# Where the second layer's w_ada tiles are loaded and summed: in passes A and B alone

## What is computed

```python
for l in range(DEPTH):
    mod = jnp.einsum('bd,dn->bn', cond, w_ada[l]) + b_ada[l]          # cond = silu(c), w_ada[l]: 1024 x 6144
    sh1, sc1, g1, sh2, sc2, g2 = [m[:, None, :] for m in jnp.split(mod, 6, axis=-1)]
    h = rms_norm(x, norm1[l]) * (1.0 + sc1) + sh1
    x = x + g1 * token_mixer(h, ...)                                  # three attention branches, gates, w_out
    h = rms_norm(x, norm2[l]) * (1.0 + sc2) + sh2
    x = x + g2 * swiglu(h, w_gu[l], w_down[l])
```

## Time and profile before

| | |
|---|---|
| median of 3 runs | 994.08 us (994.02 to 995.42) |
| the profiled execution's own time | 991.47 us |
| its span in the profile | 989.3 us |
| PE busy | 935.7 us (95%) |
| DVE busy | 694.0 us (70%) |
| ACT busy | 482.7 us (49%) |
| mean granted clock of PE | 0.976 of full |
| read from HBM | 196.24 MB |

### The profile page before, as it was taken

The page is one execution under the profiler, slowest core; times in us unless marked ns, Lnnn a source line. Parts: engine busy times, 40 slices in busy tenths (PEclk is TensorE's granted clock), DMA queues, the critical chain, the costliest instruction groups (busy, mean ns, idle before and its releaser), DMA issues.

```text
span 989.3 us, 15954 instructions
## 1 busy us (share of the span) xinstructions
PE 935.7 (95%) x6744; PEld 880.1 (89%) x6744; DVE 694.0 (70%) x1087; ACT 482.7 (49%) x654; POOL 24.4 (2%) x49
## 2 busy tenths in 40 slices
PE   8998989998998999999989998999989899999998
PEld 6787969976987999999978997898779799999998
DVE  4997889787784656666574797988878555656443
ACT  4554776455445433343463468374553454333341
POOL 1010000000000000000000000000000000000000
PEclk8999999999998999999989999999999789999999
DMA  9979633414652776767545795251454434654541
GB/s 361 384 285 373 238 114 132 171 44 171 255 213 86 256 255 216 280 237 281 181 170 183 273 327 187 92 204 45 172 211 173 171 128 171 218 207 172 178 164 43
DMA packets 29593, 198.31 MB, mean 200 GB/s; under 512 B 3282, under 2 KB 3794, under 8 KB 7507
## 3 DMA queue, kind: packets, MB, share of 16 engines
q1 hardware_dynamic: 23474, 155.22, 43.6%
q0 software_dynamic: 5760, 41.95, 11.5%
q10 hardware_dynamic: 288, 0.14, 0.0%
HBM read 196.24 MB, written 1.05 MB: 199 GB/s over the span
## 4 chain that ended last, share of the span: by engine, by line
PE 62%; DVE 24%; ACT 7%; issue 4%; DMA 3%; ACTq 0%; DVEq 0%
PE bank L479 16%; PE bank L481 16%; PE bank L480 16%; DVE w_lo L1174 7%; ACT w_hi L873 2%; DVE front L1181 2%; DVE score L1346 2%; DMA raw<-in_slabs_dram 2%; DVE acc L1437 2%; PE bank L506 1%; PE bank L586 1%; PE bank L585 1%; PE bank L587 1%; DVE score L1364 1%; ACT acc L1083 1%
## 5 line engine op out<-in xcount | busy, mean ns | idle before, releaser
L1174 DVE TENSOR_TENSOR w_lo<-raw,w_hi 128x2048 fp32r<-128x2048 f32 (+2 forms) x146 | 314.6, 2160 | 138.7 <-ACT w_hi L873 137.1
L479 PE MATMUL bank<-h_hi,w_hi 128*128 128x256 f32 x1216 | 350.8, 289 | 12.1 <-DVE w_lo L1174 6.2
L873 ACT ACTIVATE w_hi<-raw 128x2048 fp32r<-128x2048 f32 (+2 forms) x146 | 262.9, 1806 | 175.0 <-PE bank L481 120.9
L481 PE MATMUL bank<-h_hi,w_lo 128*128 128x256 f32 x1216 | 347.2, 286 | 0.0
L480 PE MATMUL bank<-h_lo,w_hi 128*128 128x256 f32 x1216 | 347.2, 285 | 0.0
L479 PEld LDWEIGHTS bank<-h_hi,w_hi 128*128 128x128 f32 x1216 | 236.5, 194 | 16.7 <-issue 14.9
L480 PEld LDWEIGHTS bank<-h_lo,w_hi 128*128 128x128 f32 x1216 | 236.5, 195 | 0.1
L481 PEld LDWEIGHTS bank<-h_hi,w_lo 128*128 128x128 f32 x1216 | 236.4, 194 | 0.0
L479 PE MATMUL bank<-y_hi,w_hi 128*128 128x256 f32 x480 | 135.6, 282 | 2.2 <-DVE w_lo L1174 2.2
L480 PE MATMUL bank<-y_lo,w_hi 128*128 128x256 f32 x480 | 135.1, 282 | 0.0
L481 PE MATMUL bank<-y_hi,w_lo 128*128 128x256 f32 x480 | 135.0, 281 | 0.0
(11 more groups left out here) (171 smaller groups left out, 1151.2 us busy)
## 6 DMA issues: line engine op xcount, KB each, us to landing
raw<-in_slabs_dram SPq DMA_DIRECT2D x124, 1024.0 KB, 5.1
front<-in_ada_dram POOLq DMA_DIRECT2D x31, 1024.0 KB, 5.7
acc<-in_ada_dram POOLq DMA_DIRECT2D x9, 1024.0 KB, 5.7
raw<-in_slabs_dram SPq DMA_DIRECT2D x16, 552.0 KB, 4.9
front<-in_ada_dram SPq DMA_DIRECT2D x5, 1024.0 KB, 11.4
raw<-in_slabs_dram SPq DMA_DIRECT2D x6, 768.0 KB, 6.7
proj<-in_ada_dram SPq DMA_DIRECT2D x2, 1024.0 KB, 9.1
x_t<-in_x_dram SPq DMA_DIRECT2D x2, 512.0 KB, 5.3
```

The costliest lines, as they stand in the source:

```text
L479: nc.tensor.matmul(b_out, st_hi, mv_hi, start=start, stop=False, skip_group_check=True)
L481: return nc.tensor.matmul(b_out, st_lo, mv_hi, start=False, stop=stop, skip_group_check=True)
L873: nc.scalar.activation(w_hi[:, n % RING, 0:w], raw[:, n % RING, 0:w], ACT.Copy).then_inc(hi_ready.sem, 1)
L1174: nc.vector.tensor_tensor(w_lo[:, n % RING, 0:w], raw[:, n % RING, 0:w], w_hi[:, n % RING, 0:w], ALU.subtract).then_inc(lo_ready.sem, 1)
```

## The change

The first layer keeps its order. In the second layer the twelve `A_B` tiles are summed after S_A+2, S_A+3, ... S_A+7 (one each, and one more after the last), S_B, S_B+1, S_B+2, S_B+3 and S_B+5, and nowhere else. They go through all three places in turn. POOL loads all twelve as places come free, with no wait for a head. ACT's wait ahead of its squares into `acc` asks for all twelve sums (before: for six).

```diff
-    ADA_SEQ += [(*_tiles[i], i % 3) for i in range(6)] + [(*_tiles[i], i % 2) for i in range(6, 12)]
+    ADA_SEQ += [(*t, i % 2 if _l == 0 and i >= 6 else i % 3) for i, t in enumerate(_tiles)]
@@ POOL
-                for _ in range(10):
+                for _ in range(12 if l else 10):
                     load_ada(n)
                     n += 1
-                pool.wait_ge(scored.sem, scored.at(l, B_HEADS + A_HEADS))
-                for _ in range(2):
-                    load_ada(n)
-                    n += 1
+                if l == 0:
+                    pool.wait_ge(scored.sem, scored.at(l, B_HEADS + A_HEADS))
+                    for _ in range(2):
+                        load_ada(n)
+                        n += 1
@@ ACT
-                act.wait_ge(ada_used.sem, KT + (24 if l else 0) + 6)
+                act.wait_ge(ada_used.sem, KT + (24 + 12 if l else 6))
@@ DVE, second layer (the branch l > 0)
                     for k in range(2, KT):
                         lo(l, S_A + k)
+                        ada_next()
+                    ada_next()
@@ DVE, both layers: the same for the calls after S_B+7, S_GATE0, S_GATE0+1, S_UQ+1 and S_UQ+2
                 lo(l, S_B + 7)
-                ada_next()
+                if l == 0:
+                    ada_next()
@@ DVE, the heads
-                    if n in (15, 17):
+                    if l == 0 and n in (15, 17):
                         ada_next()
```

## The result

The changed kernel takes 985.63 us (median of 10 runs, 984.11 to 989.99) against 994.05 us (10 runs, 990.88 to 997.10): ratio 0.9918, interval 0.9902 to 0.9934, or 8.2 us faster, where 4.8 were forecast. The time lies 1.1 us under the stated range. The profiled execution's own time is 985.63 us, its span 983.6, so 5.8 under the one profiled before.

A forecast was written before the change was run, and what follows sets the result against it. PE was taken as the bound (62% of the chain, DVE 24%), so DVE savings count only where PE waits for DVE, directly or through ACT. 3.2 + 1.6 = 4.8 us off 994.08 gives 989.2 us, range 986.7 to 991.8.

The forecast's parts named there:

- the seven sums: Second layer's pass A: seven sums of 2.41 us fit DVE's waits, hidden by PE's matmuls, at cost 0.
- my two bounds: Pass A transfers, 13.6 MB: 34.3 us at 395 GB/s, or 37.6 us at 362 GB/s; cost 0 either way.
- Behind S_UQ+1: From S_B+7 to S_UQ+2: removed sums let the second pair sum start earlier, gaining 3.2 us (bounds 0.8 and 4.8).
- In the heads: End of the heads: without step 15's sum PE's wait before the last transposes goes, gaining 1.6 us (bounds 1.4 and 2.4).
- The sum of step 17: Heads: it stands ahead of the last y_lo and w_lo of S_BR+1, wanted only at 738.5; removing it gains nothing.
- The rival of slow transfers: Pass A: transfers at 285 GB/s outlast the margin of 4.0 us, giving 999.0 us; chance 0.05.
- behind ACT and its own transfer, not behind the sum: At S_GATE0: w_lo, needed at 580.9, waits for these, so the first three removed sums give nothing.
- no longer compete with slabs, which only helps: After 561 us: tiles leave the DMA queues to slabs; no gain was counted for it.
- by 3.22 as a whole: Indexer heads, DVE full to 662: the chain of DVE behind ACT moves 3.22 us earlier, PE's gates with it.
- Behind it PE is full to 765, and DVE's merging follows PE: After the sum of step 17: PE has no gap to 765 us and DVE follows it; no further gain counted.
- more than the sum: Rival: all of three sums counts, 7.2 us, because ACT's order slackens too, giving 986.9 us; chance 0.08.
- the rival's: Changed kernel with norm idle matmuls plus four before the branches: the four's earlier cost had another cause, 984.5 us, ratio 0.9905.

The follow-up runs named there:

- x_h17: Kernel before with only the sum of head step 17 moved to pass A, that of step 15 staying: 992.05 us, ratio 0.9989.
- x_gates: Kernel before with only the sums behind S_B+7, S_GATE0 and S_GATE0+1 moved to pass A: 992.75 us, ratio 0.9995.
- after_delay: Changed kernel with four idle PE matmuls ahead of the second layer's branch projections: 989.29 us, ratio 0.9958 to the kernel before.
- after_again: The changed kernel as it is, run again beside the kernel before: 984.78 us, ratio 0.9911.
- before_p1: The kernel before, unchanged, run for a second profile: 994.65 us.
- x_uq: Kernel before with only the sums behind S_UQ+1 and S_UQ+2 moved to pass A: 990.01 us, ratio 0.9957.
- x_h15: Kernel before with only the sum of head step 15 moved to pass A, that of step 17 staying: 988.6 us, ratio 0.9965.
- before_p2: The kernel before, unchanged, run for a third profile: 989.63 us.
- heads_fill: Kernel before with idle matmuls around the second norm and only the two heads' sums moved: 983.61 us, ratio 0.9900 to the kernel before.

## Why the prediction was wrong

**Right, step by step.** Pass A took the seven sums for nothing; DVE's queue ran as laid out (w_lo of S_A+6 to S_A+7 5.34 us apart, the last with 0.64 us idle), the transfers at 378 GB/s, between my two bounds, and no PE gap. The 358 GB/s that the Trainium skill gives for HBM reads of one core ("DMA: Bandwidth & Descriptors", section "Where 436 GB/s comes from") is passed here by 6% over 34 us. Behind S_UQ+1 I had 3.2 us, the trace has 3.27, with ACT's w_hi of S_UQ+2 the next to be late, as worked out (DVE waits 1.71 for it). In the heads I had 1.6, the trace 1.48. The sum of step 17 was worth nothing, as x_h17 bears out. The rival of slow transfers did not come.

**Missed, small.** At S_GATE0 I read "behind ACT and its own transfer, not behind the sum", and priced at nothing that tiles "no longer compete with slabs, which only helps". The slab's transfer was the wait. ACT's w_hi of the two gate slabs, before and after:

```profile
575.82 1.92 ACT L873 ACTIVATE w_hi<-raw 128x2048 fp32r<-128x2048 f32 x1 [2.78 <-DMA raw<-in_slabs_dram]
580.74 1.92 ACT L873 ACTIVATE w_hi<-raw 128x2048 fp32r<-128x2048 f32 x1 [3.00 <-DMA raw<-in_slabs_dram]
```
```profile
575.97 1.92 ACT L875 ACTIVATE w_hi<-raw 128x2048 fp32r<-128x2048 f32 x1 [1.87 <-PE bank L607]
579.20 1.92 ACT L875 ACTIVATE w_hi<-raw 128x2048 fp32r<-128x2048 f32 x1 [1.32 <-PE bank L607]
```

From the first scaling of this layer's first norm to the copies of the latents it is 79.8 to 82.3 us (mean 80.8) in the eleven traces with the gates' sums in place and 79.2 to 80.1 (mean 79.8) in the six without: 0.5 in the first pair, 1.0 on the mean, where my sum has 0. By the ratio of x_gates it is 0.5 us, which cannot be told from 0. The other small one is a loss. PE, past the fifth indexer head 3.7 us earlier by its own place, stands longer at the transposes behind the indexer, and falls to the lower clock there:

```profile
PE bank L663 <- ACT acc L1048: 2.8, 1, 2.8
```
```profile
626.00:636.00 10.00, 7.69 (x52) 7.69 (x53) 9.34 (x18) 4.47 (x6) 0.00 (x0) 0.83 0.55 199
```

The wait was 1.1 us before, at full clock. All three unfilled traces of the changed kernel (after_delay too) have this fall, and it gives back 0.7 us (after_again; 1.2 in the first, which has another at 693). The wait alone does not bring it: before_p1 and x_uq wait 2.8 and 2.7 us there and keep the full clock. I had written that PE's gates move "by 3.22 as a whole".

**The step that failed** is the last of the sum: "Behind it PE is full to 765, and DVE's merging follows PE", from which I let everything after the heads shift by 4.8 us, and the line after it, which carried 4.8 us from one profiled execution to the median. Both took the second norm as a constant. It is not: undelayed, it lasts 14.0 to 14.5 us in four of six traces that keep the sum of step 15, and 10.89 in all four that move it. That is 3.1 us or more, the size of what I lacked. The page of the kernel before has the granted clock at 7 and 8 tenths in the slices from 767 to 816 us, and I did not ask what it would be after a shift. None of my rivals was this one; "more than the sum" gave 986.9 for another reason, all of three sums, which the traces refute (1.6 us of the two behind S_UQ+1 were lost to ACT, as forecast).

**Shown**: that when PE reaches the norm, and not only how much work is removed, decides here, since 1.73 us of pure delay costs the changed kernel 4.3 us in twelve executions and its trace has the long norm again. With the clock held the same delay costs 1.6 to 1.8, but the interval there still holds the rival's. **Open**: why the clock of the kernel before falls ahead of w_out's end in four of six profiles and that of the changed kernel in neither of its two; no run shows a rule for it. Single executions at 996.2 (x_h15) and 989.99 us (the changed kernel) were not profiled, so moving the sum may make the long norm rarer and not impossible. Open too is how the 8.2 us divide in the median: the terms that the traces show, 3.3, 1.5, about 1 at the gates, 0.7 to 1.2 lost behind them and 2.4 to 3.2 at the norm in most executions, come near it, each by few traces.

## What to carry to other kernels

Work moved under a PE-bound stretch was free here, with a queue that, laid out instruction by instruction, met each due time; the two terms read this way came out within 0.2 us. Where PE has a gap with a PE-bound tail behind it, look at the granted clock there before costing a shift: it is a term that differs between executions, and one profile shows only one of its values. If such a gap cannot be closed, try idle matmuls in it: in two layers they were worth 5 to 7 us here, nearly as much as the change itself. And where a slab's wait names its own transfer, ask what else is being transferred then.

## What the runs showed of the hardware

- A wait of 1.46 us and a few one-column matmuls were followed by the lower clock for 17 us (781 to 798 in the kernel before) or for 7 (785.5 to 792 in the changed one), and by either length of the norm in executions of the same kernel (14.00 in the first profile, 10.89 in before_p2). The early fall costs 2.4 to 3.2 us to the end of the span, the late one about 1.8 against a clock that holds (208.2 to 208.6 against 206.4 to 206.9 us).
- HBM reads of 128x2048 and 128x1104 tiles from two queues at once, 378 GB/s over 34 us, with landing times of 8.2 us for a slab instead of 5.2 at a DMA share of 0.56.
- Executions of the same kernel differ by 3.1 us in their first 30 us alone (before_p1, after_again and heads_fill, 6.83 us for 32 one-column matmuls, against 3.7 to 4.4 in the others).
